# Adaptive conditioning in units of 256 columns spread over other stages, and a second pass's first loads issued at the end of the first

## What is computed

```python
sc = silu(c)                                       # 9 rows: the prompt's c and 8 samples'
for l in range(2):
    mod = (sc @ ada_w[l] + ada_b[l])               # 9 x 6144
    sh1, sc1, g1, sh2, sc2, g2 = split(mod, 6)     # 1024 columns each
    h = rmsnorm(x, norm_mix_g[l]) * (1 + sc1) + sh1
    out = even_mixer(h) if l % 2 == 0 else odd_mixer(h)
    x = x + g1 * out
    h = rmsnorm(x, norm_ffn_g[l]) * (1 + sc2) + sh2
    x = x + g2 * peer(h)                           # retrieval: keys, u_tab (hidden), v_tab (outputs)
y = rmsnorm(x, norm_final_g)
```

## Time and profile before

| | us |
|---|---|
| median of 3 runs | 5538.96 (5537.46 to 5564.53) |
| profiled execution | 5535.89 |
| its span | 5534.0 |
| PE busy in the span | 4784.5 (86%) |
| DVE / ACT / POOL busy | 2916.8 / 1508.3 / 1335.5 |
| mean granted PE clock | 0.917 of full |

### The profile page before, as it was taken

One profiled execution on the slowest core, in us unless ns is written; L12 is line 12 of the kernel. 1 busy time (PEld: TensorE's weight loads), 2 busy tenths in 40 slices (PEclk: granted clock), 3 DMA queues, 4 the chain that ended last, 5 costly groups with the idle time before them and its releaser, 6 DMA issues. The chain is left out here.

```text
span 5534.0 us, 58923 instructions
## 1 busy us (share of the span) xinstructions
PE 4784.5 (86%) x22999; PEld 3837.7 (69%) x22999; DVE 2916.8 (53%) x4359; ACT 1508.3 (27%) x2797; POOL 1335.5 (24%) x571
## 2 busy tenths in 40 slices
PE   7884536659999999899998896769999999899998
PEld 2674415647788887788886364657788887788886
DVE  0115455442588883366665102762688872366665
ACT  1001100001255564222222001211255564222222
POOL 0000000000244443344443000000244443344442
PEclk9995558879999999999999997779999999999999
DMA  5210100003366686555553521003366596455552
GB/s 200 77 38 0 38 16 1 1 32 88 100 165 166 167 245 181 169 192 190 194 201 141 184 76 45 16 35 101 108 171 162 156 262 172 171 200 194 192 194 90
DMA packets 506741, 709.90 MB, mean 128 GB/s; under 512 B 47241, under 2 KB 366338, under 8 KB 485474
## 3 DMA queue, kind: packets, MB, share of 16 engines
q1 hardware_dynamic: 501858, 689.37, 39.9%
q0 software_dynamic: 4608, 16.78, 0.9%
HBM read 552.62 MB, written 149.21 MB: 127 GB/s over the span
## 5 line engine op out<-in xcount | busy, mean ns | idle before, releaser
L2024 PE MATMUL ps<-h_parts,u_parts 128*128 128x512 f32 x6144 | 1427.5, 392 | 25.5 <-PEq L1522 13.2
L2236 PE MATMUL ps<-w_parts,v_parts 128*128 128x512 f32 x6144 | 1397.4, 390 | 36.3 <-DVE w_parts L2221 36.3
L2236 PEld LDWEIGHTS ps<-w_parts,v_parts 128*128 128x128 f32 x6144 | 1156.1, 188 | 277.6 <-POOL v_parts L2207 37.1
L2024 PEld LDWEIGHTS ps<-h_parts,u_parts 128*128 128x128 f32 x6144 | 1148.8, 188 | 262.8 <-issue 15.4
L1500 POOL TENSOR_TENSOR u_parts<-u_turned,u_parts 128x1024 fp32r<-128x1024 f32 x256 | 661.7, 2585 | 2173.4 <-ACT u_parts L1495 2173.3
L2221 DVE TENSOR_TENSOR w_parts<-w_rows,w_parts 128x512 fp32r<-128x512 f32 x256 | 624.7, 2440 | 481.0 <-ACT w_parts L2200 481.0
L2207 POOL TENSOR_TENSOR v_parts<-v_rows,v_parts 128x1024 fp32r<-128x1024 f32 x256 | 615.0, 2403 | 817.7 <-ACT v_parts L2198 817.7
L194 PE MATMUL ps<-h,arena 128*128 128x264 f32 (+2 forms) x2176 | 488.2, 388 | 98.0 <-DMA arena<-in_even_w_out_dram 33.6
L2198 ACT CAST v_parts<-v_rows 128x1024 fp32r<-128x1024 f32 x256 | 269.2, 1051 | 987.7 <-PE ps L2236 962.0
L194 PEld LDWEIGHTS ps<-h,arena 128*128 128x128 f32 (+1 forms) x2176 | 412.9, 190 | 174.5 <-DMA arena<-in_even_w_out_dram 34.1
L1487 DVE STREAM_TRANSPOSE u_turned<-u_rows 128x1024 f32<-128x1024 f32 x256 | 316.9, 1238 | 275.3 <-POOL u_parts L1500 261.4
(11 more groups left out here) (472 smaller groups left out, 3920.1 us busy)
## 6 DMA issues: line engine op xcount, KB each, us to landing
u_rows<-in_peer_u_dram SPq DMA_DIRECT2D x1024, 128.0 KB, 3.6
v_rows<-in_peer_v_dram SPq DMA_DIRECT2D x128, 1024.0 KB, 4.9
hidden_tiles<-hidden SPq DMA_DIRECT2D x256, 256.0 KB, 3.4
gate_matrices<-h SPq DMA_DIRECT2D x64, 1024.0 KB, 7.1
gates<-gate_matrices SPq DMA_DIRECT2D x32, 2048.0 KB, 7.9
hidden_in<-hidden_tiles SPq DMA_DIRECT2D x256, 256.0 KB, 3.8
arena<-in_ada_w_dram SPq DMA_DIRECT2D x24, 2048.0 KB, 7.9
w_q<-in_peer_w_q_dram SPq DMA_DIRECT2D x16, 1024.0 KB, 5.9
```

Source lines behind the costliest of these rows:

```text
L2024: ins = mm(ps[:, n % 2, :], q.uTs[:, n % 3, wp, k, :], q.hs[:, xp, k, :], start=k == 0 and (wp, xp) == (0, 0), stop=k == DT - 1 and wp == 1)
L2236: ins = nc.tensor.matmul(ps[:, o, :], q.vs[:, n % 3, vp, o * P:(o + 1) * P], q.ws[:, n % 3, wp], start=n == 0 and (vp, wp) == (0, 0), stop ...
```

## The change

`conditioning` and `modulated_norm` for the mixers go. A class `Mods` makes the modulation in units of 256 columns (24 units a layer), each with a load of 1 MB on SP, 16 matmuls and two turns on PE, and a copy and two biased copies on ACT; the turn and the finish of a unit follow the making of the next. Each layer has its own `s.mods`. The units are placed so:

- first layer, units 0 to 7: loads behind c and x in `load_rows`, making inside the new `mix_norm`; 8 to 19 in `even_mix`, 20 to 23 in `mlstm_gates` (ring of 3 slots, the first three loads at the end of the projection's loads);
- second layer, units 0 to 7: loads 0 to 5 in `mlstm_samples`, units 0 to 5 in the even head norm, 6 and 7 in `rwkv_masks`; 8 to 15 in `hgrn_gates`, 16 to 19 in `hgrn_masks` (ring of 2 slots); 20 to 23 in the odd head norm (ring of 4).

The other 23 loads of `load_rows` are issued by ACT. In `mix_norm` the scalings of even tiles are ACT's. In PEER the gates' memory (`q.g`) is shared with scores, candidates and keys, v's first slots with `u_rows` and the hidden tiles' slots with `u_turned`; so two gate loads, two v loads and four hidden loads are issued by SP inside the first pass. The waits for score stores move from the end of `peer_start` to later places, DVE waits for them ahead of the first one-hot tile, and the routing plan of the samples has two more costs (2.0 and 1.5). The arenas shrink by 1 KB a partition.

```diff
+MU = 256
...
+            if ahead is not None:
+                ahead(sp)
...
+    first = [put("c", flat("c_prompt")), put("c", flat("c_sample"), 8)]
...
+    first += [(xtok[:, i, :], io["x_prompt"][0, i * P:(i + 1) * P, :]) for i in range(TT)]
+    first += [(xtok[0:B, TT, :], io["x_sample"].rearrange("b t d -> (b t) d"))]
+    loads += [(s.gate_b[:], io["mlstm_gate_b"].rearrange("o (g h) -> h (o g)", g=2)),
               (s.m_s[:], io["state_mlstm_m"].rearrange("o b h -> h (o b)"))]
...
+            for dst, src in first:
+                sp.dma_start(dst, src).then_inc(s.loaded.sem, 16)
+            for i in range(mods.count):
+                mods.load(sp, i)
+            sp.wait_ge(s.loaded.sem, s.loaded.at(16 * count))
+
+        @block.scalar
+        def _(act):
             with nc.allow_non_contiguous_dma("two small states of a few values each"):
                 for dst, src in loads:
-                    sp.dma_start(dst, src).then_inc(s.loaded.sem, 16)
+                    act.dma_start(dst, src).then_inc(s.loaded.sem, 16)
...
+class Mods:
+    def __init__(self, s, layer, first, last, ring, rows, banks):
+        self.s, self.layer, self.first, self.count = s, layer, first, last - first
+        self.ring, self.rows, self.banks, self.slots = ring, rows, banks, ring.shape[1]
+
+    def load(self, sp, i):
+        s, u, slot = self.s, self.first + i, i % self.slots
+        if i >= self.slots:
+            sp.wait_ge(s.mod_made.sem, s.mod_made.at(i - self.slots + 1))
+        sp.dma_start(self.ring[:, slot], s.io["ada_w"][self.layer][:, MU * u:MU * u + MU].rearrange(
+            "(k p) c -> p k c", p=P)).then_inc(s.mod_loaded[slot].sem, 16)
+    def make(self, pe, i):
+        s, slot = self.s, i % self.slots
+        pe.wait_ge(s.mod_loaded[slot].sem, s.mod_loaded[slot].at(16 * (i // self.slots + 1)))
+        if i >= 2:
+            pe.wait_ge(s.mod_kept.sem, s.mod_kept.at(i - 1))
+        for k in range(DT):
+            ins = s.nc.tensor.matmul(s.ps[0:NB, self.banks[i % 2], 0:MU], s.sc[:, k, :], self.ring[:, slot, k, :],
+                                     start=k == 0, stop=k == DT - 1)
+        ins.then_inc(s.mod_made.sem, 1)
+
+    def keep(self, act, i):
+        s = self.s
+        act.wait_ge(s.mod_made.sem, s.mod_made.at(i + 1))
+        if i >= 2:
+            act.wait_ge(s.mod_turned.sem, s.mod_turned.at(i - 1))
+        s.nc.scalar.copy(self.rows[:, i % 2, :], s.ps[0:NB, self.banks[i % 2], 0:MU]).then_inc(s.mod_kept.sem, 1)
+
+    def turn(self, pe, i):
+        s = self.s
+        pe.wait_ge(s.mod_kept.sem, s.mod_kept.at(i + 1))
+        if i >= 2:
+            pe.wait_ge(s.mod_done.sem, s.mod_done.at(i - 1))
+        for j in range(MU // P):
+            ins = s.nc.tensor.transpose(s.ps[:, self.banks[2 + i % 2], j * NB:(j + 1) * NB],
+                                        self.rows[:, i % 2, j * P:(j + 1) * P], s.ident[0:NB, 0:NB])
+        ins.then_inc(s.mod_turned.sem, 1)
+
+    def finish(self, act, i):
+        s = self.s
+        act.wait_ge(s.mod_turned.sem, s.mod_turned.at(i + 1))
+        for j in range(MU // P):
+            tile = (self.first + i) * (MU // P) + j
+            ins = s.nc.scalar.activation(s.mods[self.layer][:, tile, :], s.ps[:, self.banks[2 + i % 2], j * NB:(j + 1) * NB],
+                                         ACT.Identity, bias=col(s, "ada_b", self.layer * 48 + tile), scale=1.0)
+        ins.then_inc(s.mod_done.sem, 1)
...
+    def on_pe(self, pe, units):
+        for i in units:
+            self.make(pe, i)
+            if i:
+                self.turn(pe, i - 1)
+            if i == self.count - 1:
+                self.turn(pe, i)
+
+    def on_act(self, act, units):
+        for i in units:
+            self.keep(act, i)
+            if i:
+                self.finish(act, i - 1)
+            if i == self.count - 1:
...
+def mix_norm(s, layer, mods=None):
...
+                a.activation(s.sc[:], col(s, "c", 0, 72).rearrange("p (b k) -> p k b", k=DT), ACT.Silu).then_inc(
+                    s.c_ready.sem, 1)
             for k in range(DT):
+                a.activation(h[:, k, :], x[:, k, :], ACT.Square).then_inc(s.sq_ready.sem, 1)
+            act.wait_ge(s.sum_ready.sem, s.sum_ready.at(1))
+            act.wait_ge(s.root_ready.sem, s.root_ready.at(1))
+            for j in range(2):
+                ins = a.activation(s.rstd[:, parts[j]], ps[:, j, 0:widths[j]], ACT.Sqrt, bias=s.small[:, 0:1], scale=1.0 / D)
+            ins.then_inc(s.root_ready.sem, 1)
+            if mods:
+                mods.on_act(act, units)
+            act.wait_ge(s.gain_ready.sem, s.gain_ready.at(1))
+            for k in range(0, DT, 2):
+                act.wait_ge(s.xn_ready.sem, s.xn_ready.at(k + 1))
+                a.activation(h[:, k, 0:T], h[:, k, 0:T], ACT.Identity, bias=shift[:, k, 0:1], scale=s.modA[:, k, 0:1])
...
+            for k in range(DT):
+                v.tensor_tensor(h[:, k, :], x[:, k, :], s.rstd[:], ALU.mult).then_inc(s.xn_ready.sem, 1)
+            if mods:
+                dve.wait_ge(s.mod_done.sem, s.mod_done.at(mods.count))
+            v.scalar_tensor_tensor(s.modA[:], scale, 1.0, gain.unsqueeze(2).to_broadcast([P, DT, NB]),
+                                   ALU.add, ALU.mult).then_inc(s.gain_ready.sem, 1)
+            dve.wait_ge(s.gain_ready.sem, s.gain_ready.at(1))
+            dve.wait_ge(s.xn_ready.sem, s.xn_ready.at(DT))
+            for k in range(1, DT, 2):
+                v.tensor_scalar(h[:, k, 0:T], h[:, k, 0:T], s.modA[:, k, 0:1], shift[:, k, 0:1], ALU.mult, ALU.add)
+            link(v.tensor_tensor(h[:, :, T:N], h[:, :, T:N], s.modA[:, :, 1:NB], ALU.mult))
+            v.tensor_tensor(h[:, :, T:N], h[:, :, T:N], shift[:, :, 1:NB], ALU.add)
...
+    tiles_stage(s, groups, banks=2, blocks=blocks, ahead=lambda sp: [e.mods.load(sp, i) for i in range(3)])
+
+
+MIX_MODS = 12
...
+        @block.sync
+        def _(sp):
+            for i in range(3, MIX_MODS + 3):
+                e.mods.load(sp, i)
+
+        @block.tensor
+        def _(pe):
+            e.mods.on_pe(pe, range(MIX_MODS))
+
         @block.scalar
         def _(act):
+            e.mods.on_act(act, range(5))
             for k in range(8):
                 act.wait_ge(s.step_dve.sem, s.step_dve.at(k + 1))
                 nc.scalar.activation(e.qkc[:, k, :], e.qkc[:, k, :], ACT.Silu).then_inc(s.step_act.sem, 1)
+            e.mods.on_act(act, range(5, MIX_MODS))
 
...
+            e.mods.on_act(act, range(MIX_MODS, e.mods.count))
+
+        @block.tensor
+        def _(pe):
+            e.mods.on_pe(pe, range(MIX_MODS, e.mods.count))
...
+            for i in range(MIX_MODS + 3, e.mods.count):
+                e.mods.load(sp, i)
             sp.wait_ge(s.dve_chain.sem, s.dve_chain.base)
...
+            for i in range(6):
+                e.mods.load(sp, i)
             sp.wait_ge(s.step_dve.sem, s.step_dve.at(B + 1))
...
-def head_norm(s, buf, heads, gains, gate, sq):
+def head_norm(s, buf, heads, gains, gate, sq, mods, loads, units):
...
+            for i in loads:
+                mods.load(sp, i)
...
+                mods.on_act(act, units[k])
...
+                mods.on_pe(pe, units[k])
...
+            e.mods.on_pe(pe, range(6, 8))
...
-            sp.wait_ge(q.hrow_stored.sem, q.hrow_stored.at(16))
-            for i in range(4):
-                sp.wait_ge(q.sc_stored[i].sem, q.sc_stored[i].at(16 * HC // 4))
-            for i in range(2):
-                sp.wait_ge(q.ss_stored[i].sem, q.ss_stored[i].at(32))
...
+            first_gates = max((unit["flat"] + 10) // TJ, (quad_unit[QUADS - 1] + 6) // TJ)
...
+                if pair == first_gates:
+                    assert grouped == QUADS // 4
+                    for i in range(2):
+                        sp.wait_ge(q.gates_stored[i].sem, q.gates_stored[i].at(16 * QUADS // 8))
+                    sp.wait_ge(q.s_summed.sem, q.s_summed.at(B))
+                    sp.wait_ge(q.s_columns.sem, q.s_columns.at(1))
+                    for part in range(2):
+                        load_gates(s, q, sp, part)
...
+            for slot in range(2):
+                sp.wait_ge(q.turned.sem, q.turned.at(NK - TJ + TJ * slot))
+                load_v(s, q, sp, layer, slot)
+            while stored < NK - 4:
+                store_hidden(stored)
+                stored += 1
+            sp.wait_ge(q.u_ready.sem, q.u_ready.at(NK))
+            for n in range(4):
+                sp.wait_ge(q.hid_stored[n % 2].sem, q.hid_stored[n % 2].at(16 * (n // 2 + 1)))
+                load_hidden(s, q, sp, n)
...
+                if n % GJ == 0 and n >= 2 * GJ:
+                    sp.wait_ge(q.gated.sem, q.gated.at(n - GJ))
+                    load_gates(s, q, sp, n // GJ)
+                if n % TJ == 0 and n >= 2 * TJ:
                     if n >= 3 * TJ:
                         sp.wait_ge(q.v_ready.sem, q.v_ready.at(n - 2 * TJ))
```

(33 more changed lines are left out.)

243 lines of the change are left out of this document (148 added, 95 removed).

## The result

The changed kernel takes 5397.8 us (median of four runs, 5385.4 to 5405.3), the one before 5538.6; the ratio is 0.973, with a 95% interval of 0.970 to 0.976. The forecast was 5392 in a range of 5360 to 5430. The profiled execution, the slowest of the four, took 5405.3 us, 130.6 less than that of before; the forecast for it was 5389.3.

What follows compares the result with a forecast made beforehand. PE bound the conditioning, DVE the stages where PE is idle or cold, and PE idled between PEER's passes. Gains of -195.5 and costs of +48.9 net -146.6: 5535.9 to 5389.3 profiled, median 5392, range 5360 to 5430.

Steps and rivals of the forecast that it cites:

- Opening: First layer's start up to the projection's first load: transposes end at 31 as now, first load at 78.2, minus 76.5 us.
- PEER: Gap between its two passes: loads issued early save 10.0 us a layer, minus 20; price inside first pass taken as 0.
- HGRN samples: Second layer's HGRN sample stage: last ada_w load stands ahead of the state loads, plus 2 us.
- A unit, and the clock: 256 columns, 16 matmuls and two turns: 3.65 us at the high clock, 7.0 at half; a cold start costs 2.4.
- Rival 1: Clock stays at half in the filled stages, head norms and masks: plus 43 us, 5435; chance 10%.
- Second conditioning: Second layer's stretch from the last update of x, 3024.1 to 3123.4, goes entirely: minus 99 us.
- Convolution and gates: First layer's convolution with twelve units (1.7 later) and gates with four units (+3.8): plus 5.5 us.
- Head norm 1: First head norm, six units with ACT and PE in turn, DVE's last head to 658.3: plus 12.5 us.
- RWKV masks: Mask stage after the first head norm, two cold units beside 5.3 us of DVE: plus 5.7 us.
- HGRN masks: Second layer's mask stage, four units, the last two waiting for late-issued loads: plus 12 us.
- HGRN gates: Second layer's gates, eight units from a two-slot ring at a period of 4.5 us: plus 6.2 us.
- Head norm 2: Second head norm, four units in eight heads, the first free, the last three delaying the roots: plus 4 us.

Runs made afterwards that it cites:

- e1: Changed kernel plus one tiny DVE marker instruction that waits for the opening's 29 small and x loads: 5403.3 us (ratio 0.975).
- e2: Changed kernel with the opening's eight 1 MB loads issued in the norm's block, after the transposes instead of ahead of them: 5382.2 us (0.971).
- e4: Changed kernel with HGRN's ring of ada_w loads at four slots instead of two, none loaded in the masks: 5397.1 us (0.973).
- e6: Changed kernel with the two RWKV mask units moved to where RWKV's sample states are loaded, with their own two-slot ring: 5386.8 us (0.971).
- e9: Changed kernel with later opening loads, four HGRN slots, HGRN mask units in samples, and the second layer's first eight units in RWKV's samples: 5333.5 us (0.961).

## Why the prediction was right, step by step

- **The sum.** Forecast -146.6 for the profiled execution, measured -130.6. Of the 16.0 between them 17.4 are the recurrence; all other terms together are off by 1.4 the other way. No rival happened, and the largest miss had no term at all. That the other terms come to so little is luck in part: the opening and PEER gave 8.8 less than forecast, and what came out cheaper made up for it, the convolution with the prompt behind it (2.6), the HGRN samples (1.9), the second head norm (2.3) and the output projection (2.2). The median's nearness is luck too, 5.8 us above the forecast where the profiled execution is 16.0 above: the forecast put the median 3.1 above the profiled execution, and it came 7.5 below.
- **Opening**, -76.5 against -70.6. PE in the changed kernel: the end of the transposes and the first two units.

```profile
32.50 5.54 PE L233 MATMUL ps<-ident,xtok 128*128 128x128 f32 x40
...
49.74 7.08 PE L390 MATMUL ps<-w_mod,sc 128*9 128x256 f32 x32
```

  The step that failed is the end of the transposes "at 31 as now", with the small loads' landing as its only uncertainty: it came at 38.0. The bounds of -3 and +4 were set for DMA held up by 8 MB. But the block held the loads' issue as well, 20 us of SyncE, in which the last loads are issued 2.7 us apart, as fast as the ones ahead land (385 GB/s); e1 and e2 show it. The prediction counted the queue to which the loads were moved, and not the barrier behind that queue. The rest held: 46.1 us from the transposes to the projection's load, 47.2 forecast (the sums 1.4 sooner, the units 0.5 longer).
- **A unit, and the clock.** Sixteen matmuls take 3.62 us, and a unit comes every 3.77, for 3.65 forecast; a cold start cost 0.8 to 2.9, for 2.4. Rival 1 didn't happen: in the head norms the first units took 4.94 (558.08) and 4.40 and all later ones 3.62, so the pauses of 1.1 us ahead of each head's sums did not bring the clock down (0.95 granted from 558 to 592). That is against the Trainium skill's second failure mode (TensorE: Matmul & The Clock Gate) as I had applied it; in the HGRN gates a wait of 2.36 us did cost 1.7.
- **Second conditioning**, -99 against -99.7, with the warm start of the projection behind it.
- **PEER**, -20 against -17.1: the gaps gave 10.8 a layer and not 10 (7.4 are left, 8.2 forecast). What is missing, 2.2 a layer, would be the price in the first pass, taken at 0 of 0 to 3, but it is within what the stretch varies by from kernel to kernel. Where I looked for it, at tile 112, PE has no wait. There is one at the end, where a gelu waits for a store that is queued behind v rows and hidden tiles (ACT, first layer), but PE runs through it, 480 matmuls without a pause:

```profile
2264.38 0.60 ACT L2108 ACTIVATE hidden<-ps 128x512 f32<-128x512 f32 x1 [5.97 <-DMA hidden_tiles<-hidden]
```

```profile
2159.55 109.11 PE L2182 MATMUL ps<-h_parts,u_parts 128*128 128x512 f32 x480
```

- **Convolution and gates**, +5.5 against 4.9, from DVE's first instruction of the convolution (398.01 before, 326.76) to its first of the mLSTM prompt (457.15, 390.84). DVE's last instruction of the gates is at 386.18 (455.53 before), but DVE comes to the next stage 4.24 us later and not 1.20, as it waits for the units' tail:

```profile
390.84 0.23 DVE L797 TENSOR_SCALAR arena<-upper 128x128 f32<-128x128 f32 x1 [4.24 <-PEq L689]
```

- The mLSTM prompt behind it gave 1.3 back and the convolution began 0.7 sooner, two warm starts; up to 6 had been named, and 0 taken.
- **Head norm 1, RWKV masks, HGRN masks**: 12.5, 5.7 and 12 against 11.8, 5.7 and 12 (DVE's first instruction of the HGRN prompt is at 3385.3, its first of the masks at 3365.0; 3509.7 and 3501.5 before). Working the stage out as a chain over ACT and PE, instruction by instruction, was worth it; the busy times alone, six units of 3.77 beside DVE's 19.5, would have given 3 for the first.
- **HGRN gates**, +6.2 against 8.9 (7.7, and 1.2 that the projection ahead had gained). The period was taken at 4.5, between 4.1 and 4.7; measured are two units in 8.8, 10.0 and 10.7 us, so 4.4 to 5.4, and 37.1 for all eight. The Trainium skill's 6.15 us for 1 MB (DMA: Bandwidth & Descriptors, section Bandwidth) had given 8.6 and is nearer; the landing here is 5.3 in the median, and the rest is the cold unit after a wait. e4 shows that the ring's depth was the fault, not the loads' size.
- **HGRN samples** +2 against -0.6: the states' loads start when the ring lets them, and the cost was in the gates already; I had counted it twice. **Head norm 2** +4 against 1.7: three of the four units were covered, as DVE waits only once for the roots, 1.54 us ahead of the last head.

## What to carry to other kernels

- A load that is "issued early" costs its queue's time, not only the DMA's: if its block ends with a barrier, count the issue of all of them against the barrier, and put long loads where something longer runs beside.
- Place filler work by what the engine waits for: beside a wait for DMA or beside another engine's 4 us it was free (e6, e9), in a stage whose other work needs the same two engines in turn it cost 2 us a unit, and a ring of two slots cost another 7 to 9 us over twelve units (e4).
- A stage in which PE's clock goes up and down can gain or lose 17 us when anything ahead of it moves. Compare it apart from the change, and don't book it on the change.
